# Reordering the decode part of a hybrid decoder step, with half of each decode score sum moved to GpSimd

## The chip, the cores and the metric

The kernel runs on one NeuronCore of a Trainium2 chip. The metric is the device time of one execution in microseconds. The kernel before took 907.06 us (median of three runs, 905.66 to 908.23). The profile is one further execution: 907.18 us in all, of which 905.4 us is the span from its first to its last instruction.

## What is computed

One layer of a decoder, for a prompt of 512 tokens and, in the same launch, for 8 sample tokens (one new token each, with a key/value cache of 2048 rows). Cut to what matters:

```python
proj = x_ext @ w_in                                   # 1024 -> 3*512 attention columns + RWKV columns
att  = dilated_window_attention(q, k_all, v_all)      # 8 heads; cache rows with strides 1, 4 and 16
def step(S, inp):                                     # RWKV-7, 8 heads of 64, one token after the other
    sa = einsum('bhvk,bhk->bhv', S, -kk_t)
    S  = S * w_t + sa * (kk_t * a_t) + v_t * k_t
    return S, einsum('bhvk,bhk->bhv', S, r_t)
y_rw  = (group_norm(y) * gn_w + gn_b + bonus * v) * g
x1    = layer_norm(ALPHA * x + concat(att, y_rw) @ w_out)
y     = layer_norm(ALPHA * x1 + conv_ffn(x1))
```

The samples' attention needs, for each of the 8 samples, the dot products of its query with its gathered keys (three tiles of 128 rows, 8 heads of 64 columns), a softmax, and the weighted sum of its values.

## The kernel before, in words

It is one hand-ordered program: each engine has its own list of instructions, written out in the order in which it runs, and semaphores join them. There is no scheduler. Four stages follow each other.

1. Projection (to about 222 us): 27 slots of weights, TensorE nearly always busy.
2. The recurrence by chunks (about 222 to 382 us). The 512 tokens are four pairs of chunks of 64, `n` = 0 to 3 (the text calls them the first to the fourth pair). For each pair a triangular matrix is inverted in five levels, `l` = 1 to 5. A level is a ring between TensorE and VectorE: `half_products` (TensorE, into `banks`), `halves` (VectorE, `lower<-banks,level`), `full_products` (TensorE), `update` (VectorE, `xx<-xx,banks`, and `xf<-xx,banks` in level 5). The work on pair `n - 1` that follows its inverse (`value_side`, `solved`, `step_terms`, `value_terms`, `chain_step`, `state_outputs` on TensorE; `transitions`, `chain_state`, `add_y` on VectorE; `b1_copy`, `wu_copy`, `ny_copy` on ScalarE) stands between the levels of pair `n`. At the end of a pair, `inverse_start` (VectorE, `lower<-banks,causal`), `start_inverse` (TensorE) and `x0_copy` (ScalarE) prepare the next pair; `to_tokens` (TensorE) and `token_copy` (ScalarE) transpose its keys through PSUM bank 6.
3. The output projection with the group norm beside it (about 382 to 450 us for the attention half): 16 blocks `attn_out(t)` on TensorE, each added into `z` by `attn_sum(t)`. `attn_part` says which output rows and which half of the tokens a block has. Its weights come through a ring of two: `late_high(l)` on ScalarE makes the high part, `w_low(l)` on GpSimd the low part.
4. The FFN and the norms to the end.

The decode part is strewn over stage 2. For sample `b`, the sync engine's queue loads the keys into one of three buffers (`keys_of`, which waits until `s_score(b - 3)` has freed it) and the query (`query`). GpSimd multiplies keys and query in place (`products`, L694). VectorE sums each head's 64 products (`s_score`, L1432, `sscore<-kv`). With all eight done: `decode_scores`, `s_shifted`, the exponential, `s_scaled`, `decode_back`, then `decode_values(v)` on TensorE, six groups of four products against value rows that `values_of(v)` loads through two buffers. Beside it GpSimd updates the samples' RWKV state in seven steps (`step`, L705); `state_sum(0)` and `state_sum(1)` on VectorE (L1462, `ssa<-swt`) reduce it, the first before the last five steps, the second after them. The sync queue is in order too: behind the rows that wait for `state_sum(1)` (L639) stand the first weights of stage 3 (L513), the value rows for `decode_values(2)` to `(5)` (L557 to L562), and `z` (L647, L649).

## Time and profile before

| what | value |
|---|---|
| median of three runs | 907.06 us |
| profiled execution | 907.18 us, span 905.4 us |
| TensorE busy | 829.2 us (92% of the span) |
| VectorE, ScalarE, GpSimd busy | 503.1, 330.7, 259.1 us |
| granted TensorE clock, mean | 0.960 |
| bytes read from HBM | 75.87 MB |

In the page, busy time is a share of the span over all stages. The strip of 40 slices shows where TensorE is not full: slices 12 to 17 carry the digits 7, 7, 7, 7, 5 and 8, slices 22 and 23 the digits 8 and 7, and nearly all others a 9. Slices 12 to 17 (249 to 385 us) are the recurrence, slices 22 and 23 the first norm. In rows of the timeline the columns are start, duration, engine, line, operation, tiles and shapes, count, and in brackets the idle time before with what ended it.

### The profile page before, as it was taken

The page shows a single profiled execution, that of the slowest core. Times are in us where ns is not written, and L with a number is a line of the kernel's source. Part 1 is how long each engine was busy: PE and PEld are TensorE (multiplying, and loading weights), DVE is VectorE, ACT ScalarE, POOL GpSimd, SP SyncE. Part 2 cuts the span into 40 slices and gives each one's busy share as a digit, 9 for nine tenths or more (in the row PEclk, how much of TensorE's full clock was granted, in tenths as well). Part 3 has the DMA queues.
Part 4 walks back from the last instruction along what each step waited for, and adds up shares of the span by engine and source line. Part 5 has one row for each costly group of instructions (what it writes and reads, how often), then busy time and mean ns, then how long its engine had stood idle before and what let it go on. Part 6 is the DMA issues. An engine that isn't in the chain of part 4 may idle for free.

```text
span 905.4 us, 23127 instructions
## 1 busy us (share of the span) xinstructions
PE 829.2 (92%) x10012; PEld 776.0 (86%) x10012; DVE 503.1 (56%) x764; ACT 330.7 (37%) x569; POOL 259.1 (29%) x113
## 2 busy tenths in 40 slices
PE   6999999999977775899998799999999999999994
PEld 6899889888766664688987799999999999999994
DVE  5579677685658654425643477766666662000036
ACT  5644555553321212323325633333333332111124
POOL 0000000001456440214523355444444444334300
PEclk9999999999997989899998699999999999999997
DMA  8232222242535043421221033323332322223302
GB/s 260 79 93 70 92 73 72 93 155 48 141 93 163 4 131 114 133 99 53 65 85 49 24 104 109 93 93 93 94 94 94 93 88 85 85 88 95 92 2 95
DMA packets 32470, 83.47 MB, mean 92 GB/s; under 512 B 5144, under 2 KB 10456, under 8 KB 31728
## 3 DMA queue, kind: packets, MB, share of 16 engines
q1 hardware_dynamic: 32368, 81.98, 29.3%
q8 instruction: 79, 1.29, 0.6%
q14 instruction: 23, 0.19, 0.1%
HBM read 75.87 MB, written 5.91 MB: 90 GB/s over the span
## 4 chain that ended last, share of the span: by engine, by line
PE 84%; DVE 9%; ACT 3%; issue 2%; DMA 1%; SPq 1%; POOL 0%; DVEq 0%; ACTq 0%; POOLq 0%
PE banks L1796 82%; DVE sscore L1432 1%; DVE xx L1200 1%; DVE z L1203 1%; PE banks L1850 1%; DVE rw L1200 1%; DMA kv<-in_cv 1%; PE banks L2190 1%; DVE z L1200 1%; DMA att<-in_x 1%; DVE ms L1200 1%; DVE lower L1200 1%; DVE ssa L1462 1%; DVE x_lo L1200 0%; ACT x_hi L1108 0%
## 5 line engine op out<-in xcount | busy, mean ns | idle before, releaser
L1796 PE MATMUL banks<-x_hi,w_hi 128*128 128x264 f32 (+1 forms) x784 | 208.8, 299 | 14.4 <-DVE x_lo L1200 11.5
L1796 PE MATMUL banks<-x_hi,w_lo 128*128 128x264 f32 (+1 forms) x784 | 199.3, 287 | 0.0
L1796 PE MATMUL banks<-x_lo,w_hi 128*128 128x264 f32 (+1 forms) x784 | 199.2, 287 | 0.0
L1796 PEld LDWEIGHTS banks<-x_hi,w_hi 128*128 128x128 f32 x784 | 139.9, 192 | 27.5 <-issue 15.2
L676 POOL TENSOR_TENSOR w_lo<-w_raw,w_hi 128x1024 fp32r<-128x1024 f32 (+1 forms) x40 | 95.3, 2383 | 188.9 <-ACT w_hi L791 188.7
L1796 PEld LDWEIGHTS banks<-x_lo,w_hi 128*128 128x128 f32 x784 | 140.2, 193 | 0.1
L1796 PEld LDWEIGHTS banks<-x_hi,w_lo 128*128 128x128 f32 x784 | 140.0, 192 | 0.0
L676 POOL TENSOR_TENSOR wx_lo<-w_raw,wx_hi 128x1024 fp32r<-128x1024 f32 (+1 forms) x36 | 86.1, 2393 | 101.1 <-ACT wx_hi L791 100.7
L1203 DVE SCALAR_TENSOR_TENSOR z<-z,banks 128x260 f32<-128x260 f32 (+1 forms) x24 | 12.4, 516 | 118.8 <-PE banks L1796 113.3
L1796 PE MATMUL banks<-xx,lower 64*64 64x64 f32 x1280 | 56.0, 236 | 20.3 <-DVE xx L1200 16.8
L1796 PEld LDWEIGHTS banks<-xx,lower 64*64 64x64 f32 x1280 | 49.0, 146 | 29.8 <-issue 16.4
L1796 PE MATMUL banks<-x_hi,wx_hi 128*128 128x260 f32 x352 | 73.6, 283 | 0.0
L1796 PE MATMUL banks<-x_hi,wx_lo 128*128 128x260 f32 x352 | 73.5, 283 | 0.0
L1796 PE MATMUL banks<-x_lo,wx_hi 128*128 128x260 f32 x352 | 73.4, 283 | 0.0
L1203 DVE SCALAR_TENSOR_TENSOR cv<-gp,par,cv 128x544 f32<-128x544 f32 x44 | 68.3, 1553 | 1.6
L685 POOL MEMSET kv<- 32x1536 f32 x3 | 4.1, 1372 | 219.7 <-PE banks L1796 219.5
L1200 DVE TENSOR_TENSOR h_lo<-hh,h_hi 128x520 fp32r<-128x520 f32 x22 | 51.5, 2339 | 23.7 <-ACT h_hi L1145 23.7
L791 ACT ACTIVATE w_hi<-w_raw 128x1024 fp32r<-128x1024 f32 (+1 forms) x40 | 41.6, 1039 | 45.8 <-PE banks L1796 44.9
L1796 PEld LDWEIGHTS banks<-x_hi,wx_hi 128*128 128x128 f32 x352 | 55.4, 188 | 0.2
L1796 PEld LDWEIGHTS banks<-x_hi,wx_lo 128*128 128x128 f32 x352 | 55.4, 188 | 0.0
L1796 PEld LDWEIGHTS banks<-x_lo,wx_hi 128*128 128x128 f32 x352 | 55.2, 188 | 0.0
L791 ACT ACTIVATE wx_hi<-w_raw 128x1024 fp32r<-128x1024 f32 (+1 forms) x36 | 37.3, 1037 | 46.5 <-PE banks L1796 44.8
(257 smaller groups left out, 1721.2 us busy)
## 6 DMA issues: line engine op xcount, KB each, us to landing
w_raw<-in_w SPq DMA_DIRECT2D x87, 512.0 KB, 3.6
w_raw<-in_w SPq DMA_DIRECT2D x16, 448.0 KB, 3.4
kv<-in_ck SPq DMA_DIRECT2D x16, 192.0 KB, 3.4
kv<-in_cv SPq DMA_DIRECT2D x16, 192.0 KB, 3.6
att<-in_x SPq DMA_DIRECT2D x8, 264.0 KB, 6.3
att_out<-att SPq DMA_DIRECT2D x1, 2112.0 KB, 9.0
z<-in_xc SPq DMA_DIRECT2D x2, 1040.0 KB, 9.5
y_out<-z SPq DMA_DIRECT2D x8, 260.0 KB, 2.2
```

Of the source, the lines that this page charges most:

```text
L676: pool.tensor_tensor(lo[:, 0:n * P], w_raw[:, s % 2, 0:n * P], hi[:, 0:n * P].bitcast(F32), ALU.subtract)\
L685: pool.memset(kv[96:P, r * NSB * AW:(r + 1) * NSB * AW], 0.0).then_inc(kv_zero, 1)
L791: ac.activation(w_at(l)[0][:, 0:n * P], w_raw[:, s % 2, 0:n * P], ACT.Copy).then_inc(w_hi_ready, 1)
L1200: return ve.tensor_tensor(out, a0, a1, op)
L1203: return ve.scalar_tensor_tensor(out, a0, s, a1, op0, op1)
L1432: ve.tensor_reduce(sscore[:, :, b * H:(b + 1) * H], kv[:, r * NSB * AW:(r + 1) * NSB * AW].rearrange("p (t h d) -> p t h d", t=NSB, d=HD), ...
L1462: ve.tensor_reduce(ssa[:, i, :], swt[:, :, :], AX, ALU.add).then_inc(sw_y if i else sw_sa, 1)
L1796: return pe.matmul(out, l, r, start=start, stop=stop)
L1850: ins = pe.transpose(banks[:, 4 - p, j * P:(j + 1) * P], sw[:, u % 4, j * P:(j + 1) * P], ident[:, :])
L2190: ins = pe.transpose(banks[:, 6, c * P:(c + 1) * P], x[:, c, n * P:n * P + P], ident[:, :])
```

## The change

It computes the same. On GpSimd each product is followed by a second instruction that adds the upper 32 columns of each head onto the lower 32, and VectorE sums 32 values in place of 64. The eight sums move: two to the end of the first pair, three to the end of the second, one each into levels 2, 3 and 5 of the third. The bonus products (`bonus`) go two at a time into levels 3 and 4 of the first pair, with banks of their own; the bias on ScalarE that follows them moves into the next pair. `state_sum(0)` moves from the third pair to level 3 of the second, `state_sum(1)` from level 2 of the fourth to level 3; the softmax moves from the third pair into the fourth. `transitions` and `value_terms` move back by one place each, `chain_state` to level 5 and after the last update. At a pair's end the first half of the next inverse starts before the second transposition, and the three transpositions come in another order. `decode_values(0)` to `(2)` stand in the fourth pair, `(3)` to `(5)` in stage 3. The queue loads `z` before the value rows. In stage 3 the blocks run through four output rows of one half, then four of the other.

```diff
-J_V, J_K, J_KK, J_R = (3 + i * CC for i in range(4))
+J_V, J_KK, J_K, J_R = (3 + i * CC for i in range(4))
@@ attn_part
-        return 2 * (t // 4) + t % 2, t // 2 % 2
+        return 4 * (t // 8) + t % 4, t // 4 % 2
@@ sync
-        for v in range(2, 6):
-            values_of(v)
         sp.wait_ge(bt_ps, 3 * TB - 2)
         sp.dma_start(z[:, 0:CC, :], a["xc"][:, 0:CC, :]).then_inc(z_landed, 16)
+        values_of(2)
+        values_of(3)
         sp.wait_ge(bt_ps, 3 * TB - 1)
         sp.dma_start(z[:, CC:KT, :], a["xc"][:, CC:KT, :]).then_inc(zb_landed, 16)
+        values_of(4)
+        values_of(5)
@@ gpsimd, products
-                .then_inc(s_prod, 1)
+                .then_inc(q_used, 1)
+            own(q_used)
+            x = kv[:, r * NSB * AW:(r + 1) * NSB * AW].rearrange("p (g d) -> p g d", d=HD)
+            pool.tensor_tensor(x[:, :, 0:HD // 2], x[:, :, 0:HD // 2], x[:, :, HD // 2:HD], ALU.add).then_inc(s_prod, 1)
@@ scalar, late_high
-                ac.wait_ge(o_ps, min(4 * (l - 1), 2 * KT))
+                ac.wait_ge(o_ps, (6, 8, 14, 16, 2 * KT, 2 * KT)[l - 2] if l < L_RW + 2 else 2 * KT)
@@ scalar, pairs
+            if n < TB - 1:
+                token_copy(n, 0)
+                x0_copy(n + 1, 0)
+                token_copy(n, 1)
+                x0_copy(n + 1, 1)
+                token_copy(n, 2)
...
+        ac.activation(rw[:, J_G:J_G + 2, :], rw[:, J_G:J_G + 2, :], ACT.Sigmoid).then_inc(lo_act, 1)
@@ vector, pairs
-                if (n, l) == (0, 5):
-                    s_score(0)
-                if n == 1:
-                    s_score(l)
-                if (n, l) == (2, 1):
+                if n >= 1 and l == 4:
+                    transitions(n - 1)
+                if (n, l) == (1, 3):
                     state_sum(0)
-                if n == 2 and l in (2, 3):
-                    s_score(l + 4)
-                if (n, l) == (2, 4):
+                if n == 2 and l in (2, 3, 5):
+                    s_score((5, 6, 6, 7)[l - 2])
+                if (n, l) == (3, 1):
                     s_shifted()
                 if (n, l) == (3, 2):
+                    s_scaled()
+                if (n, l) == (3, 3):
                     state_sum(1)
...
             if n >= 1:
+                chain_state(2 * n - 1)
                 add_y(n - 1)
+            if n == 0:
+                s_score(0)
+                s_score(1)
+            if n == 1:
+                s_score(2)
+                s_score(3)
+                s_score(4)
@@ tensor, end of a pair
+            if n < TB - 1:
+                inverse_scores(n + 1, 0)
+                to_tokens(n, 0)
+                full_products(n, NLEV - 1, 0)
+                inverse_scores(n + 1, 1)
+                if n >= 1:
+                    chain_step(2 * n - 1)
+                full_products(n, NLEV - 1, 1)
+                start_inverse(n + 1, 0)
+                to_tokens(n, 1)
+                if n >= 1:
+                    state_outputs(n - 1)
+                start_inverse(n + 1, 1)
+                to_tokens(n, 2)
+                if n == 2:
+                    decode_scores()
```

VectorE, from level 5 of the first pair to level 1 of the second, in the kernel before:

```order
L1432 TENSOR_REDUCE sscore<-kv 128x3x8
L1200 TENSOR_TENSOR xf<-xx,banks 128x256
L1200 TENSOR_TENSOR lower<-banks,causal 128x2x2x128
L1200 TENSOR_TENSOR xf<-xx,banks 128x256
L1200 TENSOR_TENSOR lower<-banks,causal 128x2x2x128
L1200 TENSOR_TENSOR rw<-banks,rw 128x528
L1200 TENSOR_TENSOR lower<-banks,level 128x4x64 x2
```

The same place on VectorE in the kernel after:

```order
L1214 TENSOR_TENSOR xf<-xx,banks 128x256
L1214 TENSOR_TENSOR lower<-banks,causal 128x2x2x128
L1214 TENSOR_TENSOR xf<-xx,banks 128x256
L1214 TENSOR_TENSOR lower<-banks,causal 128x2x2x128
L1447 TENSOR_REDUCE sscore<-kv 128x3x8 x2
L1214 TENSOR_TENSOR lower<-banks,level 128x4x64 x2
```

The sum `sscore<-kv` stood ahead of the last update; now two stand behind it, and the last bonus row (`rw<-banks,rw`) is gone from the end.

VectorE in the kernel after, from level 5 of the second pair into level 1 of the third:

```order
L1417 COPY carry<-nv 128x256
L1214 TENSOR_TENSOR xf<-xx,banks 128x256
L1214 TENSOR_TENSOR lower<-banks,causal 128x2x2x128
L1214 TENSOR_TENSOR xf<-xx,banks 128x256
L1214 TENSOR_TENSOR lower<-banks,causal 128x2x2x128
L1217 SCALAR_TENSOR_TENSOR carry<-banks,dec,nv 128x64 x4
L1214 TENSOR_TENSOR yy<-yy,banks 128x4x64
L1447 TENSOR_REDUCE sscore<-kv 128x3x8 x3
L1214 TENSOR_TENSOR lower<-banks,level 128x4x64 x2
```

In the kernel before each of the five levels of this pair had one such sum, and none stood at its end.

ScalarE in stage 3 of the kernel before, from the square of the first group-norm unit to its root (`w_hi` is `late_high(2)`, `gsd` the root):

```order
L1053 ACTIVATE mixa_hi<-banks 128x4x8
L1057 ACTIVATE yy<-banks 128x4x8
L1031 ACTIVATE gsq<-banks 128x512
L949 ACTIVATE nv<-banks,dec 128x64 x8
L954 ACTIVATE yy<-banks 128x4x64 x2
L791 ACTIVATE w_hi<-w_raw 128x1024
L1040 ACT_TABLE_LOAD
L1040 ACTIVATE gsd<-banks,par 128x128
```

The same in the kernel after:

```order
L1045 ACTIVATE gsq<-banks 128x512
L954 ACTIVATE nv<-banks,dec 128x64 x8
L959 ACTIVATE yy<-banks 128x4x64 x2
L1069 ACTIVATE mixa_hi<-banks 128x4x8
L797 ACTIVATE w_hi<-w_raw 128x1024
L1054 ACT_TABLE_LOAD
L1054 ACTIVATE gsd<-banks,par 128x128
```

The samples' attention rows (`mixa_hi`) now stand behind the ten copies of the last pair (`nv`, `yy`), directly ahead of `w_hi`, which in its turn waits for six output blocks in place of four.

## Rows read from the trace of the kernel before

**Rows 1.** Page: what ended last, by engine and by line.
```profile
PE 84%; DVE 9%; ACT 3%; issue 2%; DMA 1%; SPq 1%; POOL 0%; DVEq 0%; ACTq 0%; POOLq 0%
```
**Rows 2.** Windows: span; busy of PE, PEld, DVE, ACT, POOL; clock; DMA share; GB/s.
```profile
253.00:288.00 35.00, 23.51 (x787) 21.14 (x785) 21.08 (x31) 7.21 (x17) 18.26 (x6) 0.85 0.36 112
288.00:329.00 41.00, 29.53 (x958) 26.61 (x953) 27.08 (x43) 9.14 (x24) 25.71 (x7) 0.88 0.36 105
```
**Rows 3.** Waits of PE, 222 to 480 us: total, times, longest.
```profile
PE banks L1796 <- DVE xx L1200: 16.8, 12, 3.8
PE banks L1796 <- DMA kv<-in_cv: 9.2, 1, 9.2
PE banks L1796 <- issue: 4.1, 5, 1.8
```
**Rows 4.** Timeline of DVE, first to second pair.
```profile
251.41 0.42 DVE L1200 TENSOR_TENSOR xf<-xx,banks 128x256 f32<-128x256 f32 x1
...
262.35 0.42 DVE L1200 TENSOR_TENSOR lower<-banks,level 128x256 f32<-128x256 f32 x1 [7.87 <-PE banks L1796]
```
**Rows 5.** DVE groups by form, 222 to 382 us: count, busy and mean, idle.
```profile
L1432 DVE TENSOR_REDUCE sscore<-kv 128x24 f32<-128x1536 f32 x8 | 14.0, 1753 | 0.3
L1462 DVE TENSOR_REDUCE ssa<-swt 128x32 f32<-128x2048 f32 x2 | 4.6, 2286 | 0.1
```
**Rows 6.** Timeline of DVE, third pair.
```profile
300.12 0.42 DVE L1200 TENSOR_TENSOR lower<-banks,level 128x256 f32<-128x256 f32 x1 [3.35 <-PE banks L1796]
...
317.87 1.41 DVE L1200 TENSOR_TENSOR xx<-xx,banks 128x512 f32<-128x512 f32 x2
...
325.93 0.69 DVE L1200 TENSOR_TENSOR xx<-xx,banks 128x512 f32<-128x512 f32 x1 [2.75 <-PE banks L1796]
328.52 0.69 DVE L1200 TENSOR_TENSOR xx<-xx,banks 128x512 f32<-128x512 f32 x1 [1.90 <-PE banks L1796]
...
341.91 0.42 DVE L1200 TENSOR_TENSOR lower<-banks,level 128x256 f32<-128x256 f32 x1 [3.08 <-PE banks L1796]
```
**Rows 7.** Timeline of DVE, fourth pair.
```profile
367.14 0.69 DVE L1200 TENSOR_TENSOR xx<-xx,banks 128x512 f32<-128x512 f32 x1 [11.82 <-PE banks L1796]
...
381.49 0.69 DVE L1200 TENSOR_TENSOR yy<-yy,banks 128x512 f32<-128x512 f32 x1 [1.44 <-PE banks L1796]
```
**Rows 8.** Windows around the wait for the value rows, columns as in rows 2.
```profile
353.00:364.00 11.00, 1.78 (x94) 1.66 (x91) 1.05 (x3) 0.00 (x0) 0.00 (x0) 0.76 0.87 260
```
**Rows 9.** POOL groups by form, 222 to 400 us, columns as in rows 5.
```profile
L694 POOL TENSOR_TENSOR kv<-kv,qs 128x1536 f32<-128x1536 f32 x8 | 27.6, 3447 | 32.1 <-DMA kv<-srow 22.0 <-issue 9.5 <-DMA qs<-q_rows 0.5
L705 POOL TENSOR_TENSOR swt<-w_raw,svec 128x2048 f32<-128x2048 f32 x2 | 9.2, 4603 | 1.0 <-DMA sval<-sixr 0.9
L676 POOL TENSOR_TENSOR w_lo<-w_raw,w_hi 128x1024 fp32r<-128x1024 f32 x2 | 4.8, 2391 | 50.6 <-ACT w_hi L791 50.5
L734 POOL TENSOR_TENSOR gw_gate<-gsb,rw 128x512 f32<-128x512 f32 x1 | 1.3, 1265 | 0.1
```
**Rows 10.** Timeline of SP and POOL, keys of sample 4 and its product.
```profile
267.18 0.35 SPq L529 DMA_DIRECT2D kv<-in_ck  x1
272.00 3.44 POOL L694 TENSOR_TENSOR kv<-kv,qs 128x1536 f32<-128x1536 f32 x1 [9.53 <-issue]
```
**Rows 11.** Timeline of ACT and PE, stage 3.
```profile
396.19 0.43 PE L1796 MATMUL banks<-mixa_hi,w_hi 128*128 128x260 f32 x1 [0.73 <-DVE mixa_lo L1200]
...
404.31 1.89 ACT L949 ACTIVATE nv<-banks,dec 128x64 f32<-128x64 f32 x8 [1.46 <-PE banks L1796]
...
407.06 1.06 ACT L791 ACTIVATE w_hi<-w_raw 128x1024 fp32r<-128x1024 f32 x1
...
410.96 0.79 PE L1796 MATMUL banks<-grs,gsel 128*128 128x128 f32 x5 [1.00 <-issue]
```
**Rows 12.** Timeline of DVE and POOL, 439 to 443 us.
```profile
439.59 2.40 POOL L676 TENSOR_TENSOR w_lo<-w_raw,w_hi 128x1024 fp32r<-128x1024 f32 x1 [3.01 <-ACT w_hi L791]
440.20 2.34 DVE L1200 TENSOR_TENSOR gyc<-gyc,gw_gate 128x512 f32<-128x512 f32 x1
```

214 lines of the change are left out of this document (108 added, 106 removed).

## The prediction

> **What bounds the kernel now.** I read the chain that ended last first: 84% of it is TensorE [rows 1], so only time in which TensorE stands idle, or in which its work is stretched, can be won. The windows say where that is: TensorE is busy 23.5 of 35 us from 253 to 288 and 29.5 of 41 us from 288 to 329 [rows 2]. No engine is full there: VectorE has 21.1 and 27.1 us. It is a ring, TensorE and VectorE waiting for each other in turn, so whatever VectorE does between `halves` and `update` is paid in full. The waits confirm it: 16.8 us of TensorE's idle time end with `xx` of VectorE, 9.2 us in one piece with the value rows, 4.1 us with nothing that the profile shows [rows 3]. In the fourth pair VectorE then waits 11.8 us for TensorE [rows 7], and in that stretch the DMA engines move 260 GB/s at a share of 0.87 [rows 8]: it is a real queue of bytes, started late, not a slow transfer. The change works almost wholly inside the recurrence, so I walk through its four pairs from mark to mark (the first `halves` of a pair on VectorE) and then through stage 3.
>
> **Prices.** A sum of 1536 values takes 1.753 us and one of 2048 takes 2.286 us [rows 5], 1.04 ns for each value more; 768 values then take 0.95 us. The half addition on GpSimd handles 768 values; it is not in the trace. The 128x512 row takes 1.27 us and the 128x1024 row 2.39 us [rows 9], which are its bounds; halfway, and by the product's rate (3.447 us for 1536), it is about 1.75 us. Eight are 14 us more on GpSimd, beside other engines' work. A sample's keys take 4.8 us from the first issue (267.18) to the start of the product (272.00) [rows 10].
>
> **First pair to second.** The last `xf` starts its chain at 251.41 and the second pair at 262.35, after VectorE has been idle for 7.87 us [rows 4]. That idle time is a detour: bonus 3 on VectorE, its bias on ScalarE, only then the token copies, and only behind them the next inverse. All of that leaves the path. The bonus products cost TensorE the same, two at a time; with the sum of 1.75 us gone from level 5, `xf` comes at about the old time (I take 0.9 us later, since two bonus products of some 1.1 us each now stand ahead of one `half_products`). From `xf` to the next mark I take 4.7 us: two updates with their masks 2.3 us and the 3.1 to 3.4 us that VectorE waits at the other pair ends [rows 6], less 0.9 us because the two halves of the start overlap. The mark moves from 262.35 to 257.0: 5.3 us won. The two half sums (1.9 us) fit into that wait.
>
> **Second pair (37.8 us, 262.35 to 300.12).** Five sums of 1.753 + 0.03 us go: 8.9 us. `state_sum(0)` comes in, 2.3 us [rows 5]. Three half sums stand at the end, 2.9 us. The wait there was 3.35 us [rows 6], but with the last `chain_state` (0.9 us) behind the update too and the next inverse begun sooner, only about 1 us of cover is left: 1.9 us are paid. Moving `transitions` under the wait for `full_products` gives 1.9 us. Sum: 6.6 us won, 31.2 us left. If all three were covered it would be 8.5 us.
>
> **Third pair (41.8 us, 300.12 to 341.91).** `state_sum(0)` goes, 2.3 us. Two sums become three half sums: 3.5 us against 2.9 us, 0.6 us. The softmax steps go to the fourth pair, 1.7 us. The keys of samples 5, 6 and 7 can only be fetched once the sums at the end of the second pair have freed their buffers. That gives product 5 at about +4.8 us, and its halves after 3.45 + 1.75 us: 10.0 us behind the first of the three sums. VectorE reaches `s_score(5)` 2 x 0.95 + 3.0 + 4.3 = 9.2 us behind it, so it waits 0.9 us; the next two products (5.2 us each) keep pace with a level of 5.2 us. What is left is level 4: from the third `update` (317.87) to the fourth it takes 8.06 us, and the fourth's second half comes 2.6 us later still (328.52) [rows 6], because `transitions` stands ahead of `halves` and `value_terms` ahead of `full_products`. With both moved, level 4 is 1.41 + 0.1 + 0.9 + 1.85 = 4.3 us; `value_terms` is then paid before level 5, about 2 us. Together with `chain_state` out of the start of level 5 I take 7.8 us. Sum: 2.3 + 0.6 + 1.7 - 0.9 + 7.8 = 11.5 us won, 30.3 us left.
>
> **Fourth pair (39.6 us, 341.91 to 381.49).** The 11.8 us of waiting go [rows 7]. It is covered now because sums, steps and `state_sum(1)` end some 17 us sooner and because `decode_values(2)` stands behind the pair's last level. Behind `state_sum(1)` the queue now has two weights (1.05 MB), half of `z` (1.04 MB) and the value rows (0.79 MB): 2.9 MB at 260 GB/s [rows 8] are 11 us, after 1.5 us for the issues, so the rows land 13 us after the sum. TensorE comes to them 4.3 + 10 us behind it: just covered, with about 1 us to spare. To pay: the softmax, 1.7 us, and 0.5 us for its second step. That step (`s_scaled`) reads and writes only SBUF, and the GpSimd steps run beside it. One row shows what that can cost: `gyc<-gyc,gw_gate` takes 2.34 us and ends just behind `w_lo` of GpSimd [rows 12], where it otherwise takes 0.69 us. The bounds are 0 and one whole step, 4.6 us [rows 9]. Sum: 11.8 - 1.7 - 0.5 = 9.6 us won.
>
> The Trainium skill, SBUF — State Buffer, "Who interferes with whom", says that VectorE and GpSimd share one pair of ports as an exclusive lock, which a scalar operation in a two-port mode or an instruction with two SBUF inputs takes, while a reduction never does. By it the half sums stay free of the longer GpSimd work and only `s_scaled` can be held; by a rule without the lock the fourth pair would be 0.5 us shorter. The trace agrees for the row of 2.34 us.
>
> The four together: 5.3 + 6.6 + 11.5 + 9.6 = 33.0 us.
>
> **Stage 3.** Here I see losses. TensorE's fourth to sixth value group (one of them new here) adds 1.0 us. `mixa_hi` now stands on ScalarE behind the ten copies of the last pair (1.89 + 0.8 us) [rows 11], and the fifth block waits for it: about 2.1 us against the 0.73 us of the third block before. Then `late_high(2)` (1.06 us) waits for six blocks, not four, and the first root stands behind it. `gn_spread(0)`, which follows the sixth block on TensorE, waited 1.00 us [rows 11]. Now the chain is weight copy 1.06, table load 1.28, root 0.37, reciprocal 0.95 us = 3.7 us behind the sixth block, with about 1 us of `chain_step` and `state_outputs` over it: 2.8 us. Sum: 1.0 + (2.1 - 0.7) + (2.8 - 1.0) = 4.2 us lost. `z` comes sooner, which ends a wait of VectorE alone. The later weights come at about the old places.
>
> **The clock.** My walk takes TensorE's rows at 2.4 GHz. The granted clock was 0.85 and 0.88 in the two windows [rows 2], that is, part of them ran at 1.2 GHz, each time after a stretch in which TensorE had little to do; such stretches will remain. `value_terms` is now on the path in three pairs, and at 1.2 GHz it is some 2 us longer. And 1.8 us of unexplained waiting once stood in the third pair [rows 3]. I take 4 us off (bounds 0 and 10).
>
> Result: 33.0 - 4.2 - 4 = 24.8 us. The profiled execution's 907.18 us (0.12 us from the median of 907.06 us) becomes 882.4 us; I forecast 882.
>
> **Rivals.**
> 1. *The ring closes wholly.* Dense work keeps the clock at 2.4 GHz and the ScalarE waits in stage 3 are absorbed: 33.0 us, 874 us. For it: the longest idle stretches, before which the clock fell, are those that go. Against it: the waits on `xx` of 3.8 us [rows 3] come before level 2, which the change leaves as it is.
> 2. *The wait moves on.* The value rows arrive late after all, behind 1.04 MB of `z` more, or the reordered levels in the third pair bring only half of their 7.8 us. Losing 4 us there, 4 us in the third pair and 5 us more to the clock leaves 12 us: about 895 us. For it: my cover for the rows is 1 us; the 7.8 us are measured in a stretch that also had a slow clock.
> 3. *GpSimd becomes the bound, and the kernel is slower.* VectorE runs in order, so if product and half addition are slow, it stands at `s_score(5)`, `(6)` and `(7)` in levels 2, 3 and 5 of the third pair with all levels queued behind it, and each microsecond more for a half addition is paid three times. From 1.75 + 24.8 / 3 = 10 us for one half addition on the kernel is slower than before; at 12 us it would be 913 us. For it: nothing but that the operation (two inputs from one tile, in strips of 32) is not in the trace. Against it: rows of comparable size take 1.27 to 2.39 us [rows 9].
> 4. *The change does not do what it says*: the three sums at the end stop the chain for all of their 2.9 us and the other sums wait for their products, so that moving wins nothing. Even then the first pair, level 4 and the wait for value rows are left; this lies within rival 2.
>
> **How the numbers follow.** Forecast, 876 to 889 us: 0.60. Rival 1, under 876: 0.15. Rivals 2 and 4, 889 to 904: 0.18. Rival 3, slower: 0.05. No change within 0.3% (2.7 us, about what a measurement of this kernel can tell from none): 0.02. So faster 0.93, same 0.02, slower 0.05. The range reaches to 871 us, which takes in most of rival 1, and to 896 us, most of rival 2; it leaves out about 0.15.
>
> **What would show it.** After: VectorE idle between the last `xf` of the first pair and the next `halves` about 2 us instead of 7.9; sums of 0.95 us; half additions of 1.75 us; pairs of 31, 30 and 30 us; no wait over 2 us on value rows; the third pair's `s_score(5)` waiting about 1 us for GpSimd; two waits of TensorE of 2 to 3 us in stage 3; the projection and the FFN unchanged. I am wrong if a wait on `kv` or `sscore` of more than 5 us appears, or if the third pair is still over 35 us.

## The result, and the profile after

The changed kernel took 894.07 us (median of four, 892.27 to 897.88), the kernel before 907.19 us beside it: a ratio of 0.9862, 95% interval 0.9825 to 0.9899. I had forecast 882 us. The kernel is faster by 13.1 us, about half of the 24.8 us that I had worked out; the interval shows a gain of 1.0 to 1.8%. What came is the size of rival 2 ("the wait moves on", 895 us).

The profiled execution took 897.88 us (span 896.1), 9.3 us less than before's 907.18. A second profile of the same kernel, e1_after, shows 892.73 us (span 890.9); where the two differ I give both. The walk by the forecast's marks:

| us | before | forecast | after | e1_after |
|---|---|---|---|---|
| mark of the second pair | 262.35 | 257.0 | 257.80 | 256.96 |
| second pair | 37.8 | 31.2 | 34.1 | 32.0 |
| third pair | 41.8 | 30.3 | 38.6 | 38.3 |
| fourth pair, to the last `yy` | 39.6 | 30.0 | 33.6 | 32.0 |
| stage 3, to the first `lst<-banks` | 77.5 | 81.7 | 85.9 | 86.1 |
| the rest | 446.4 | 446.4 | 446.1 | 445.6 |

Each mark but the first and last is a row `lower<-banks,level` of VectorE. The first row of the table came true, the second within the spread of two profiles; the third pair and stage 3 did not. The profiled execution was forecast at 882.4 us. Of the 15.5 us by which it missed, the third pair has 8.3, stage 3 4.2, the fourth pair 3.6 and the second 2.9, less the 4 us that I had set aside for the clock.

The chain that ended last, answering to [rows 1]; the shares by engine:

```profile
PE 84%; DVE 6%; issue 5%; ACT 4%; POOL 1%; DMA 0%; DVEq 0%; ACTq 0%; POOLq 0%
```

VectorE's share fell from 9% to 6%, as wanted, but "issue" rose from 2% to 5%. TensorE's waits from 222 to 480 us [rows 3] say the same:

```profile
PE banks L1813 <- DVE xx L1214: 14.6, 11, 4.6
PE banks L1813 <- issue: 11.6, 8, 2.5
...
PE banks L1813 <- DVE z L1217: 1.3, 1, 1.3
...
PE banks L1813 <- DVE mixa_lo L1214: 1.0, 1, 1.0
PE banks L1813 <- DVE grs L1561: 0.9, 1, 0.9
PE banks L1813 <- ACT gsq L1045: 0.9, 1, 0.9
```

The 9.2 us for value rows are gone. 11.6 us now end with nothing that the profile names, where it was 4.1 us, and the last four rows are stage 3's (at 387 us, and from 424 to 428 us). The same windows as [rows 2], then that of [rows 8]:

```profile
253.00:288.00 35.00, 27.64 (x965) 24.43 (x962) 22.43 (x41) 11.18 (x24) 18.67 (x6) 0.95 0.20 57
288.00:329.00 41.00, 28.92 (x1008) 26.59 (x1003) 24.43 (x46) 7.95 (x20) 32.37 (x11) 0.88 0.42 128
353.00:364.00 11.00, 8.58 (x204) 6.98 (x195) 3.35 (x12) 5.34 (x13) 4.79 (x2) 0.84 1.02 340
```

TensorE is busier in the first of them (27.6 us against 23.5) and no busier in the second (28.9 against 29.5), where its clock is still 0.88 on average. In the third it works beside the transfers, where it stood before.

VectorE at the end of the first pair [rows 4] and the sums [rows 5]:

```profile
253.28 0.42 DVE L1214 TENSOR_TENSOR xf<-xx,banks 128x256 f32<-128x256 f32 x1 [0.18 <-PE banks L1813]
253.73 0.69 DVE L1214 TENSOR_TENSOR lower<-banks,causal 128x512 f32<-128x512 f32 x1
254.46 1.94 DVE L1447 TENSOR_REDUCE sscore<-kv 128x24 f32<-128x768 f32 x2
257.80 0.89 DVE L1214 TENSOR_TENSOR lower<-banks,level 128x256 f32<-128x256 f32 x2 [1.40 <-PE banks L1813]
```
```profile
L1447 DVE TENSOR_REDUCE sscore<-kv 128x24 f32<-128x768 f32 x8 | 7.6, 953 | 3.4 <-POOL kv L701 3.2
```

The idle time of 7.87 us has become 1.40 us, and a sum takes 0.953 us (0.95 forecast). The third pair [rows 6]:

```profile
288.92 2.93 DVE L1447 TENSOR_REDUCE sscore<-kv 128x24 f32<-128x768 f32 x3
291.88 0.88 DVE L1214 TENSOR_TENSOR lower<-banks,level 128x256 f32<-128x256 f32 x2
...
297.63 0.42 DVE L1214 TENSOR_TENSOR ms<-banks,causal 128x256 f32<-128x256 f32 x1
301.26 0.95 DVE L1447 TENSOR_REDUCE sscore<-kv 128x24 f32<-128x768 f32 x1 [3.21 <-POOL kv L701]
...
320.24 0.89 DVE L1214 TENSOR_TENSOR lower<-banks,level 128x256 f32<-128x256 f32 x2 [3.60 <-PE banks L1813]
```

The reader is to see two things: no idle time ahead of 291.88, so the three sums are partly paid, and 3.21 us at the sum of sample 5. The other side of that wait, on the sync queue and on GpSimd [rows 9, 10]:

```profile
289.94 0.35 SPq L530 DMA_DIRECT2D kv<-in_ck  x1
```
```profile
295.85 3.45 POOL L697 TENSOR_TENSOR kv<-kv,qs 128x1536 f32<-128x1536 f32 x1 [23.79 <-issue]
299.38 1.78 POOL L701 TENSOR_TENSOR kv<-kv 128x768 f32<-128x768 f32 x1
```

The keys are asked for when the first of the three sums has ended (289.87), and the product starts 5.9 us later. The half addition takes 1.78 us (1.75 forecast). TensorE's clock in the same pair, columns as in [rows 2]:

```profile
299.70:303.00 3.30, 0.01 (x2) 0.01 (x2) 1.67 (x3) 0.00 (x0) 3.22 (x2) 0.69 0.59 157
303.00:307.70 4.70, 4.70 (x136) 4.70 (x139) 1.56 (x4) 0.00 (x0) 4.54 (x3) 0.50 1.01 297
```

TensorE stands through the whole of the first window. It had stopped at 298.44 already and goes on at 302.99, 4.6 us in all (the longest of the waits on `xx` above). The granted clock fell to 0.50, its 1.2 GHz, at 301.0, while it stood, and stayed there until 307.8, so that the 4.8 us of work behind the wait ran at it. The fourth pair [rows 7]:

```profile
340.05 0.41 DVE L1463 TENSOR_SCALAR qs<-qs,sstat 64x384 f32<-64x384 f32 x1
...
351.48 1.41 DVE L1214 TENSOR_TENSOR xx<-xx,banks 128x512 f32<-128x512 f32 x2
358.60 0.89 DVE L1214 TENSOR_TENSOR lower<-banks,level 128x256 f32<-128x256 f32 x2 [5.71 <-PE banks L1813]
...
364.10 0.69 DVE L1214 TENSOR_TENSOR yy<-yy,banks 128x512 f32<-128x512 f32 x1
```

The 11.82 us wait is now one of 5.71 us at level 5, and 2.42 of these are TensorE's own unexplained wait:

```profile
358.05 0.91 PE L1813 MATMUL banks<-xx,lower 64*64 64x64 f32 x22 [2.42 <-issue]
```

Stage 3 [rows 11], TensorE's two waits and ScalarE between them:

```profile
387.42 0.56 PE L1813 MATMUL banks<-mixa_hi,w_hi 128*128 128x260 f32 x1 [1.03 <-DVE mixa_lo L1214]
...
397.56 1.13 PE L1813 MATMUL banks<-grs,gsel 128*128 128x128 f32 x8 [2.47 <-issue]
```
```profile
386.43 0.20 ACT L1069 ACTIVATE mixa_hi<-banks 128x32 fp32r<-128x32 f32 x1
393.67 1.06 ACT L797 ACTIVATE w_hi<-w_raw 128x1024 fp32r<-128x1024 f32 x1 [7.04 <-PE banks L1813]
394.74 1.28 ACT L1054 ACT_TABLE_LOAD   x1
396.04 0.37 ACT L1054 ACTIVATE gsd<-banks,par 128x128 f32<-128x128 f32 x1
```

The 2.47 us are put down to "issue", but the chain behind them is plain: weights, table, root, then the reciprocal on VectorE. This is the loss that the forecast named (2.8 - 1.0 us). From 386.30 to 393.13 us the clock is halved as well, and there the forecast had nothing; columns as above:

```profile
386.30:393.10 6.80, 5.77 (x30) 5.45 (x27) 1.37 (x6) 0.30 (x2) 0.00 (x0) 0.50 0.01 2
```

The wait of 1.03 us lies from 386.39 to 387.42. So the clock had fallen 0.09 us before it began (0.45 us before it in e1_after), and 5.7 us of work behind it ran at half the clock. TensorE had been busy without a pause from 380 us on, part of the time with thin products: 16 products of 4 columns each took 1.95 us from 383.48 on.

### The profile page after: what moved, and what is told of

Its sections match the earlier page's. It is cut to its first block, busy times and chain, and to the rows that moved or that the text cites. A ratio compares the mean times of both kernels' runs of the same rounds, so it can differ in the third digit from the quotient of the medians.

```text
span 896.1 us, 23137 instructions
## 1 busy us (share of the span) xinstructions
PE 825.6 (92%) x10012; PEld 773.6 (86%) x10012; DVE 495.5 (55%) x764; ACT 330.8 (37%) x569; POOL 273.8 (31%) x121
## 4 chain that ended last, share of the span: by engine, by line
PE 84%; DVE 6%; issue 5%; ACT 4%; POOL 1%; DMA 0%; DVEq 0%; ACTq 0%; POOLq 0%
PE banks L1813 81%; PE banks L1867 1%; ACT z L1125 1%; ACT x_hi L1122 1%; DVE xx L1214 1%; DVE z L1214 1%; DVE rw L1214 1%; DVE z L1217 1%; PE banks L2216 1%; DVE ms L1214 1%; ACT z L1185 0%; DMA w_raw<-in_w 0%; POOL kv L697 0%; DVE lower L1214 0%; POOL x_lo L749 0%
## 5 line engine op out<-in xcount | busy, mean ns | idle before, releaser
L679 POOL TENSOR_TENSOR wx_lo<-w_raw,wx_hi 128x1024 fp32r<-128x1024 f32 (+1 forms) x36 | 86.1, 2392 | 102.3 <-ACT wx_hi L797 101.9
```

What stands on the lines that cost most here:

```text
L679: pool.tensor_tensor(lo[:, 0:n * P], w_raw[:, s % 2, 0:n * P], hi[:, 0:n * P].bitcast(F32), ALU.subtract)\
```

## A wait that the profile calls issue

Of 11.6 us only the 2.47 us above are explained by a semaphore. For the others I looked at the queue that the profile's table lists as "q8 instruction", beside the data queue, as a share of the same 16 DMA engines. It moves packets of 16384 bytes: 79 packets in the whole program. The views of the transfers in two neighbouring stretches of after, first 347.2 to 355.4 us, then 355.4 to 356.6 us (kind: packets, MB, share of the engines):

```profile
q1 hardware_dynamic: 589, 2.17, 72.3%
```
```profile
q1 hardware_dynamic: 204, 0.36, 98.4%
q8 instruction: 1, 0.02, 5.2%
```

No such packet moves while 2.17 MB of weights and `z` do, then one does (355.52 to 356.51), and TensorE resumes at 358.05, 1.54 us later. In the profiles of all kernels here there are 89 waits of this kind of more than 0.25 us between 222 and 382 us; in each, TensorE resumes 1.22 to 1.70 us behind the end of such a packet. It looked as if TensorE ran out of instructions. The experiments e6, e9 and e10 are about that.

## The experiments

All are edits of the changed kernel, except e16. Each was timed beside the kernel before, whose medians were 905.9 to 906.6 us. The spread of one kernel over a handful of runs is 2 to 10 us, so a part is judged by its stretch of the profile, and the whole by the ratio.

**e1_after**: the changed kernel again.

> The changed kernel once more, beside the three that follow, so that they are compared on one chip. Both theories expect 892 to 898 us. The late-keys theory expects VectorE to wait about 3.2 us for GpSimd ahead of the sum of sample 5 again. The bytes theory expects the waits of TensorE that end with nothing the profile shows (1.98 us near 310, 2.42 us near 358) to stand at the same places.

893.19 us (892.0 to 893.7), ratio 0.9853 [0.983, 0.9877]. The third pair and stage 3 repeat to 0.3 us; the second and fourth differ by 2.1 and 1.6 us between the two profiles.

**e2_spread**: the sums of samples 2 and 3 go into levels 1 and 2 of the second pair.

```diff
+                if n == 1 and l in (1, 2):
+                    s_score(l + 1)
...
             if n == 1:
-                s_score(2)
-                s_score(3)
                 s_score(4)
```

> In the second pair the sums of samples 2 and 3 stand in levels 1 and 2 and only sample 4's at the end; all else as in the changed kernel. Theory A (late keys: the three sums at the end free the key buffers too late, VectorE waits 3.2 us at sample 5, TensorE idles 4.5 us and its clock is halved for 6.8 us after it): the second pair pays 2 x 0.98 us in its levels and gets about 2 us back at its end; product 5 comes some 25 us sooner, the wait of 3.2 us goes, the slow stretch after it too; the third pair falls from 38.6 to 32 to 34 us and the kernel is 4 to 6 us faster. Rival B (bytes: the third pair is long because TensorE's instructions arrive late behind loads): the third pair stays at 36 us or more, the kernel gains at most 2 us.

891.07 us (890.72 to 897.05), ratio 0.9845 [0.9817, 0.9873]. The wait at sample 5 is gone:

```profile
297.08 0.42 DVE L1214 TENSOR_TENSOR ms<-banks,causal 128x256 f32<-128x256 f32 x1
297.54 0.95 DVE L1447 TENSOR_REDUCE sscore<-kv 128x24 f32<-128x768 f32 x1
```
```profile
290.47:323.02 32.55, 25.02 (x981) 22.45 (x976) 21.15 (x42) 7.42 (x19) 26.17 (x7) 1.00 0.36 112
```

The third pair takes 32.55 us in place of 38.3 to 38.6, at a clock of 1.00 throughout (0.87 in after, 0.91 in e1_after): 5.7 to 6.0 us less, and 32.5 to 33.1 us in the three later kernels with this edit. This is the main error of the forecast. Counted from the start of the pair, VectorE comes to the sum of sample 5 2.3 us sooner than in after (3.4 than in e1_after), and from that sum to the end of the pair 3.7 us (2.4) are won behind it. That second part holds the halved clock and also TensorE's waits for instructions, which are 1.8 us in this pair against 3.2 and 2.5.

The edit takes away the wait and two of the three sums ahead of it at once, and the wait alone isn't the whole cause. In e7_dv below the clock falls early in the pair already (it is 0.75 from 293 to 300 us), the wait is short, and the pair still takes 38.6 us:

```profile
298.36 0.95 DVE L1447 TENSOR_REDUCE sscore<-kv 128x24 f32<-128x768 f32 x1 [1.08 <-POOL kv L701]
```

The whole kernel was expected 4 to 6 us faster and the medians show 2.1, with intervals that overlap those of e1_after. The fourth pair takes 34.1 us (33.6 and 32.0 without the edit), with an unexplained wait of TensorE of 3.4 us instead of 2.3 to 2.4, and stage 3 0.5 to 0.7 us more.

**e3_root**: `gn_root(0)` stands ahead of `late_high(2)` on ScalarE.

```diff
-        late_high(2)
         gn_root(0)
+        late_high(2)
         gn_high(0)
```

> On ScalarE the first root of the group norm stands ahead of the third weight's high part, not behind it. Theory A (stage 3 loses because the root waits for six output blocks): the reciprocal no longer ends 2.5 us of TensorE's idle time, 3 to 4 us are won. Rival B (other work fills the place, or the weight then comes late): under 1 us.

893.18 us (887.52 to 897.21), ratio 0.9841 [0.9805, 0.9877]. Stage 3 goes from 85.9 to 82.7 us in the profile and the 2.47 us wait is gone. The whole kernel doesn't show the 3 to 4 us expected: the median is that of e1_after, with six runs spread over 9.7 us.

**e4_loads**: the gate weights are issued behind the state rows, and the first half of `z` behind the value rows.

```diff
-        sp.dma_start(gate_up[:], a["gate_up"]).then_inc(gate_landed, 16)
...
         values_of(2)
         values_of(3)
         sp.wait_ge(bt_ps, 3 * TB - 1)
+        sp.dma_start(z[:, 0:CC, :], a["xc"][:, 0:CC, :]).then_inc(z_landed, 16)
```

> Only the order of loads is changed: the gate weights and two selectors (1 MB) are loaded behind the first two groups of value rows instead of behind the last keys, and the first half of z (1.04 MB) behind the value rows of groups 2 and 3 and the second transposition of the fourth pair. Theory A (bytes: the loads in one burst delay the fetch of TensorE's instructions): the waits of 1.98 us near 310 and of 2.42 us near 358 that nothing in the profile ends shrink below 0.7 us each, 3 to 5 us are won, unless z is then late. Rival B (these waits belong to TensorE's own stream): they stay at 1 to 2.5 us wherever the loads stand, and the time is the same within 1 us.

893.68 us (891.77 to 897.31), ratio 0.9863 [0.9838, 0.9889]: no change. The wait of 1.98 us near 310 us is gone, and the third pair still takes 37.6 us; that of the fourth pair stays (2.97 us, with 1.82 MB ahead of the packet): two weight tiles and the value rows do what `z` did.

**e5_fullsum**: no half additions, sums of 64 values.

```diff
-                .then_inc(q_used, 1)
-            own(q_used)
-            x = kv[:, r * NSB * AW:(r + 1) * NSB * AW].rearrange("p (g d) -> p g d", d=HD)
-            pool.tensor_tensor(x[:, :, 0:HD // 2], x[:, :, 0:HD // 2], x[:, :, HD // 2:HD], ALU.add).then_inc(s_prod, 1)
+                .then_inc(s_prod, 1)
```

> The reordered kernel without the half additions: GpSimd does the product alone, VectorE sums 64 values again (1.75 us a sum in place of 0.95). It isolates what the half sums on GpSimd bring. Theory A (what I hold: the ring pays each sum that VectorE does between its masks and updates, and the third pair waits for the product of sample 5, whose keys can only be fetched once the three sums have ended): the three sums at the end of the second pair cost 2.4 us more, and the keys of sample 5 are fetched 0.8 us later at the first free buffer; product 5 is ready 1.8 us sooner behind its keys because the half addition is gone, so the wait of 3.2 us at the sum of sample 5 goes down to about 3.2 - 1.8 + 0.8 - 2.4, nothing; the three sums in the third pair cost 2.4 us more. Second and third pair together 2.4 + 2.4 - 3.2 = 1.6 us longer, the first pair 1.6 less its cover: 0 to 1.6 us. Total +1.5 to +3 us against the reordered kernel, about 895 us against 893.5. Theory B (the half sums carry the gain, GpSimd's work is hidden): 8 x 0.8 = 6.4 us longer, 900 us. Theory C (the half additions hold the chain: the product chain of GpSimd is the bound of the third pair): it is faster, 890 us.

897.04 us (895.84 to 897.46), ratio 0.9892 [0.9862, 0.9921], 3 to 4 us above the changed kernel; the intervals of the ratios just overlap. The wait for GpSimd at sample 5 is gone, and the third pair is 37.4 us, at a clock of 0.82. The time lies between theory A (895 us) and B (900), nearer to A; C (890) is out.

**e6_shift and e9_half**: the first group of value scores is computed nine times and five times in place of once, which moves everything behind it against the edges of TensorE's packets.

```diff
-            for c in range(CC):
+            for c in [i for _ in range(9 if (n, p) == (0, 0) else 1) for i in range(CC)]:
```

> The reordered kernel with the first group of value scores of the first pair computed nine times in place of once on TensorE: 64 matrix products of 64x64 more, all before the second pair, same result. They cost 3 to 6 us in the first pair and do nothing for the rest. Theory F (the waits of TensorE that end with nothing the profile shows are waits for the next packet of its instructions, of 16384 bytes, that is for each 128 pairs of weight load and product): the places of the packets move by half a packet against the program, so the waits of 2.0 us at 310, 1.2 us at 319, 1.2 us at 333 and 2.4 us at 358 are gone from the instructions before which they stood, others stand some 64 products earlier in the program, and each still ends 1.3 to 1.6 us behind the end of such a packet. Rival G (these waits are for semaphores or a data transfer which the profile does not attribute): they stand before the same instructions as before, of the same size within 0.3 us.

The wait near 310 us stands before the same instruction, and so do those near 319, 333 and 358 us. But I had counted 64 more products, and the page shows 128 (10140 for 10012) and 80 packets for 79. That is one packet for 256 instructions, 64 bytes each, and the edges lay where they had lain: the run could not tell the theories apart. It did give the size of a packet. So I ran it again with half of that.

> The reordered kernel with the first group of value scores of the first pair computed five times in place of once on TensorE. The run with nine had 128 more pairs of weight load and product (10140 against 10012), that is one whole packet of 16384 bytes more (80 against 79), so the packets' edges lay at the same instructions again and it told nothing. Here it is 64 pairs more: half a packet. Theory F (TensorE's unexplained waits stand at the edges of its instruction packets): the waits inside value_terms of the third pair and before the last products xx,lower of levels 3 and 5, which stood before the same instructions in both earlier runs, are gone from there; waits of 0.5 to 3 us stand 64 pairs earlier or later in the program, each ending 1.3 to 1.6 us behind the end of a packet. Rival G (a semaphore or a transfer): same instructions as before.

894.1 us, one run. With 64 products more, TensorE's waits from 305 to 312 us are

```profile
PE banks L1813 <- DVE xx L1214: 1.1, 1, 1.1
```

in place of, in after,

```profile
PE banks L1813 <- issue: 2.0, 1, 2.0
PE banks L1813 <- DVE xx L1214: 0.4, 1, 0.4
```

The wait inside `value_terms` near 319 us has gone as well; others of 0.43 and 0.94 us have come at 318.7 and 324.2 us, before `rw,aa` and `level,lower`, where none stood. A wait of 1.60 us at 357.83 is also before an `xx,lower`, but not before the one of after: it is the 5288th product of the program, where that of after (358.05) is the 5161st and would be the 5225th here. Numbered by product modulo 128, all 89 waits stand at places 59 down to 31, the later in the program the lower, and none anywhere else. No semaphore and no data has changed, only the count of instructions ahead. Rival G falls: these waits are TensorE waiting for its next 256 instructions.

**e7_dv**: the first two value groups of the fourth pair go behind the `half_products` of levels 4 and 5.

```diff
+                if n == 3 and l >= 4:
+                    decode_values(l - 4)
...
-                    decode_values(0)
-                if (n, l) == (3, 4):
-                    decode_values(1)
```

> The reordered kernel, but the first two groups of the value products of the samples in the fourth pair stand behind the half_products of levels 4 and 5 in place of ahead of them, so that VectorE can work beside them. Theory P (in the ring a value group of about 1.0 us ahead of half_products is paid in full, behind it it lies beside VectorE's masks): the fourth pair is 1 to 2 us shorter than in the reordered kernel and VectorE's wait of 5.7 us at level 5 shrinks to 4 to 5 us. Rival F2 (the fourth pair is bound by the instruction packets of TensorE that wait behind the bulk transfers): the pair keeps its length within 0.5 us since the packet comes no sooner. Total 892.5 us by the first, 893.5 by the second.

897.34 us (893.24 to 898.41), ratio 0.9891 [0.9858, 0.9923]. The fourth pair takes 35.0 us, not less; TensorE's wait for instructions is 3.46 us where it was 2.42. Theory P is wrong here. I read it so that what TensorE does ahead of the packet is cover for it; no run shows that by itself.

**e8_terms**: `value_terms` goes behind `half_products` of level 5 in three pairs.

```diff
-                if n >= 1 and l == 4:
+                if n >= 1 and l == 5:
                     if n >= 2:
                         chain_step(2 * n - 2)
                     value_terms(n - 1)
```

> The reordered kernel, but value_terms (128 products of 64x64, about 2.1 us at full clock) and the chain step ahead of it stand behind half_products of level 5 in place of ahead of it, in the second, third and fourth pair. Theory P (what my forecast had: where value_terms stands it is paid before level 5, about 2 us a pair, here 1 to 1.5 us a pair of it lie beside VectorE's two masks of level 5): 3 to 4.5 us faster, about 889.5 us; each of the three pairs is 1 to 1.5 us shorter. Rival Q (chain_state stands ahead of VectorE's last updates and waits for the copies of value_terms on ScalarE, so a later value_terms only moves the wait from the masks to that place): the time stays within 1 us.

903.51 us (898.79 to 907.87), ratio 0.9973 [0.9949, 0.9997]: 10 us slower than the changed kernel, which neither theory had. The place is Q's, the size is not:

```profile
360.70 0.86 DVE L1217 SCALAR_TENSOR_TENSOR carry<-banks,dec,nv 128x64 f32<-128x64 f32 x4 [7.44 <-ACT nv L954]
```

`chain_state` needs the copies `nv` of ScalarE, which need the whole of `value_terms`; with it behind `half_products`, VectorE stands for it for 3.5, 1.8 and 7.4 us in the three pairs. Of the 7.4 us, 4.0 are a wait of TensorE for instructions inside `value_terms`, so not all of the loss is the order's own. The pairs take 35.8, 36.5 and 38.3 us: the second and the fourth are longer, the third is 2 us shorter. Of the two places tried, that of the changed kernel is the cheaper one.

**e10_throttle**: the sync queue waits for each of the two late weight tiles before it goes on.

```diff
-        weights(N_IN)
-        weights(N_IN + 1)
+        for l in range(2):
+            weights(N_IN + l)
+            sp.wait_ge(w_landed[(N_IN + l) % 2], 16 * ((N_IN + l) // 2 + 1))
```

> The reordered kernel with one thing more: in the fourth pair the sync queue waits for the first late weight tile (0.52 MB) to land before it issues the second, and for the second before it goes on to z and the value rows. The same bytes are moved. Theory F (the packet with TensorE's next instructions is served only behind the bytes that are queued ahead of it: 2.2 MB between the packets at 347.0 and 355.5, DMA engines full from 350 on): the packet comes about 3 us sooner, the wait of 2.4 us before the products of level 5 is gone or under 1 us, and the halved clock behind it is shorter; the fourth pair is 2 to 4 us shorter than 33.6 (32.0 in the second run of the same kernel), total 1 to 3 us less than the reordered kernel's 893.5, unless the value rows come later than decode_values(2) needs them. Rival H (TensorE stood there for the masks of level 5 anyway, the packet is hidden by that): the fourth pair stays within 1 us, and the value rows, 1 to 2 us later, may cost that much.

900.36 us (897.05 to 903.75), ratio 0.9934 [0.9909, 0.9959]: slower than the changed kernel. But the fourth pair takes 29.66 us, what the forecast had. TensorE from 347 to 358 us:

```profile
PE banks L1814 <- DVE rw L1215: 1.2, 1, 1.2
PE banks L1814 <- DVE xx L1215: 1.1, 1, 1.1
PE banks L2217 <- ACT yy L960: 0.5, 1, 0.5
```

No "issue" is left, with the same bytes in the same order. The packet that moved at 355.52 in after moves at 352.33 here. So Theory F's other half holds too: the packet is late when the bulk data is queued ahead of it. What is won is then lost at the value rows, which come late behind tiles and `z`:

```profile
365.79 1.94 PE L1814 MATMUL banks<-kv,sprob 128*32 128x512 f32 x8 [5.72 <-DMA kv<-in_cv]
```

The changed kernel has no such wait, so my cover for these rows held there, and this used it up. Stage 3 takes 96.0 us in place of 85.9: more than the 5.7 us, with the clock at 0.50 from 361.8 to 372.0 us.

**e11_sums**: e3_root, and the samples' sums stand ahead of `value_terms` on TensorE, `mixa_hi` ahead of the ten copies on ScalarE, `mixa_lo` ahead of `chain_state` on VectorE.

```diff
         attn_out(3)
-        value_terms(TB - 1)
         decode_sums()
+        value_terms(TB - 1)
...
         gn_square(0)
-        ny_copy(TB - 1)
         ac.wait_ge(s_sum, 1)
...
         own(s_mix_hi)
+        ny_copy(TB - 1)
```

> Stage 3 of the reordered kernel with two changes: the group norm's first root stands ahead of late_high(2) on ScalarE (as in e3_root), and the samples' attention sums stand ahead of value_terms on TensorE, with mixa_hi ahead of the ten copies on ScalarE and mixa_lo ahead of chain_state on VectorE. Theory S (my forecast's: the fifth block waits for mixa_lo because mixa_hi stands behind the ten copies of 1.89 + 0.8 us; the halved clock of the 6.7 us behind that wait follows from it): the wait of 1.0 us is gone, and with it up to 3.4 us of halved clock; stage 3 from the last add of the recurrence to the first norm goes from 82.7 us (e3_root) to 79 to 81.5 us. Rival T (the ten copies, now behind mixa_hi, hold up the chain of states and so gn_var): another wait of the same size takes its place, and stage 3 stays at 82 to 84 us.

887.02 us (885.48 to 889.69), ratio 0.9793 [0.977, 0.9816]. Stage 3:

```profile
361.11:440.54 79.43, 76.55 (x910) 66.25 (x910) 37.08 (x67) 25.11 (x45) 24.87 (x16) 0.98 0.25 79
```

79.4 us at a clock of 0.98, where e3_root had 82.7 at 0.94. With a wait of 1.0 us gone 3.3 us are won; the rest is the low clock from 386.3 us on, of which nothing is left here. That is what theory S expected (79 to 81.5 us), not T (82 to 84). But the edit also moves the thin products ahead of the wait (`par,srow`) to another place, and the clock had fallen before the wait began; which of the two the low clock belongs to isn't shown.

**e12_best**: e2, e11, e10 and the gate weights of e4 together.

> The combination: sums of samples 2 and 3 in levels 1 and 2 of the second pair (e2_spread), the root and the attention sums as in e11_sums, the gate weights issued behind the state rows (part of e4_loads), the late weights one after the other (e10_throttle). If the parts are independent: e2_spread 2 us, stage 3 3.4 to 6 us, the waits near 308 and 355 about 2 us each: 884 us, 881 to 889. Rival: each wait that goes lets another one through (fetch or clock), as in e2_spread, where 6 us won in the third pair left 2 us in all: about 889 us.

894.26 us (889.05 to 896.65), ratio 0.9857 [0.9827, 0.9886]: above both the 884 us of the parts' sum and the rival's 889. The 5.7 us for value rows are there again.

**e13_vfirst**: e11 with e10's waits, and the value rows ahead of `z`. **e14_nothrottle**: e11 with e2 and the gate weights of e4. **e15_best**: all of these.

```diff
+        values_of(2)
+        values_of(3)
         sp.wait_ge(bt_ps, 3 * TB - 2)
         sp.dma_start(z[:, 0:CC, :], a["xc"][:, 0:CC, :]).then_inc(z_landed, 16)
-        values_of(2)
-        values_of(3)
```

> e11_sums with the late weight tiles loaded one after the other as in e10_throttle, and with the value rows of the third and fourth value group ahead of the first half of z in the queue. Theory F: as in e10_throttle the packet of instructions comes in time, the wait before the products of level 5 (3.2 us in e11_sums) is gone and the fourth pair is 30 to 31.5 us (34.4 in e11_sums); the 5.7 us that TensorE stood for value rows in e10_throttle came from z (1.05 MB, 4 us) ahead of them, so 0 to 1.7 us are left. Total 884 to 886 us, against 887.0 of e11_sums. Rival: z now lands late and attn_sum(0) waits for it, which holds up TensorE's third block; the time stays at 887 or above.

892.15 us (888.51 to 894.18), ratio 0.985 [0.9822, 0.9878]. In the profile (888.83 us) the fourth pair is 29.9 us and 1.8 us of wait for value rows are left, slightly over what was expected; but stage 3 takes 83.7 us where e11 has 79.4, which is nearly all that the fourth pair had won (34.4 to 29.9), and the median is 5 us above e11's 887.02.

> e11_sums with the sums of samples 2 and 3 in levels 1 and 2 of the second pair (e2_spread) and the gate weights behind the state rows (part of e4_loads), no change to the late weights. If the parts add: third pair 32 to 34 us in place of 38, the wait before level 5 in the fourth pair stays at 2.5 to 4 us; 884 to 886 us. If the fetch gives the gain back as in e2_spread: 886 to 889 us.

886.09 us (884.54 to 888.14), ratio 0.9783 [0.9761, 0.9806]: the fastest version by its median, though no clear step from e11_sums (887.02 us): the 5.3 us won in the third pair are 0.9 us in the whole. Third pair 32.5 us, stage 3 79.4 us, the fourth pair 33.3 us with TensorE's wait of 3.2 us still in it.

> Both together: e14_nothrottle with the late weights one after the other and value rows ahead of z. Third pair 32 to 34, fourth pair 30 to 31.5, stage 3 79 to 81 us: about 881 us (878 to 885). Rival: the value rows, behind the gate weights now (0.3 us of bytes more), are waited for again by more than 2 us: 885 or more.

889.24 us (880.93 to 891.35), ratio 0.9806 [0.9772, 0.984]. The profiled execution, 880.93 us, has pairs of 32.6, 32.6 and 29.0 us; the five others took 888 to 891. Against the profile of e14_nothrottle the fourth pair wins 4.3 us and stage 3 loses 3.6 (82.95 us against 79.38), with 2.2 and 0.8 us of waits for the loads of `kv` in it. What the five others lose beyond that has no trace. So the waits on the sync queue do away with TensorE's wait for instructions before level 5 and still do not pay; a part of the loss is in stage 3, the rest stays open.

**e16_halfonly**: the kernel before with the half sums alone.

```diff
+            own(q_used)
+            x = kv[:, r * NSB * AW:(r + 1) * NSB * AW].rearrange("p (g d) -> p g d", d=HD)
+            pool.tensor_tensor(x[:, :, 0:HD // 2], x[:, :, 0:HD // 2], x[:, :, HD // 2:HD], ALU.add).then_inc(s_prod, 1)
```

> The kernel before with the half sums alone: each product on GpSimd followed by the half addition (1.80 us), each sum on VectorE of 32 values (0.95 us in place of 1.75), everything else at its old place. By the walk of my forecast: five sums in the second pair and one at the end of the first 0.8 us each, 4.8 us, and two in the third pair 1.6 us; but GpSimd's chain of steps is 14.4 us longer, state_sum(1) and with it the weights and the value rows behind it come later where the fourth pair already waited 9.2 us for them. GpSimd had 9.5 us of idle time for the products in which it waited for nothing shown, the rest is waits for keys, which come 0.8 us a sample sooner. Theory V (the value rows set the end of the recurrence in the kernel before): the rows come 2 to 6 us later, minus the 6.4 us that the sums give: the time is within 3 us of before (904 to 909). Rival W (the sums are paid one by one in the ring): 900 to 901 us.

901.56 us (898.6 to 906.48), ratio 0.9955 [0.9934, 0.9975]: 4.4 us from the half sums alone, and 3 to 4 us by e5. The second pair is 32.6 us (37.8 before), the third 40.0 (41.8); the fourth stays at 39.8 us (39.6 before) with 8.9 us of wait for value rows, but starts sooner. Rival W is the nearer. Of the 13 us, then, about 4 are the half sums' and about 9 the order's.

## Why the prediction was right in part and wrong in size

**First pair to second: right.** 5.3 us forecast, 4.6 and 5.4 measured; both sums lie in the wait.

**Second pair: nearly right.** 6.6 us forecast, 3.7 and 5.8 measured. The mark at 291.88 has no idle time ahead of it, so the three sums are paid in part, as assumed. The two profiles differ by 2.1 us, and over the seven profiles whose kernels are the same up to here the pair takes 31.0 to 35.2 us; my 31.2 is at the lower end.

**Third pair: this step failed.** I had 30.3 us and got 38.6. The wait at `s_score(5)` was sized at 0.9 us and was 3.21. VectorE came to it 9.1 us behind the start of the sums (288.92 to 298.05), as forecast (9.2). The product was late: I let the keys be fetched from the start of the first sum, but its buffer is free when it has ended, 1.0 us on, and the keys took 5.9 us and not 4.8. The step "so it waits 0.9 us" thus missed 2.3 us, 2.1 of them in these two points; and the walk had no term for what comes with such a stop. e2_spread took the wait and two of the sums ahead of it away and won 5.7 to 6.0 us. Of the 2.2 us by which its pair is still over the forecast, waits for instructions are 1.8 us (the longer two 0.43 and 1.17). Level 4 itself came as forecast: in e2_spread from its third `update` at 303.63 to its fourth at 308.18, 4.55 us against 4.3.

**Fourth pair: right in its mechanism, short by 2 to 3.6 us.** The value rows no longer hold it, `s_scaled` took 0.41 us and was not held (the GpSimd steps had ended), so its 0.5 us were nothing. What was missing is the wait for instructions behind 2.2 MB of loads, which now run beside TensorE's levels, where in the kernel before TensorE stood for the value rows anyway; e10_throttle, without that wait, shows 29.66 us against the 30.0 forecast.

**Stage 3: the mechanism right, the term half its size.** 4.2 us forecast, 8.4 measured. Root behind the weight copy: 1.8 us forecast, 3.2 by e3_root. The wait on `mixa_lo`: 2.1 us forecast, 1.03 measured, but 3.3 us by e11_sums, low clock included. The remaining loss, 79.4 us against 77.5, is 1.9 us where the new value group had 1.0.

**The clock.** I took 4 us as one lump. It comes in single stretches: 4.6 us of standing and then 4.8 us of work at 0.50 in the third pair, 5.7 us of work at 0.50 behind the wait in stage 3. In the third pair the clock fell while TensorE stood, in stage 3 just before it did. The lump of 4 us was no estimate of these.

**The rivals.** Rival 2 had the size. Its cause was another: no value row came late, and level 4 came as priced (4.55 us against 4.3; the 7.8 us as a whole no run singles out). The loss lay at the sample sums, the clock and the instructions, and that it added up to rival 2's 895 us is chance. Rival 3 was wrong in size (1.8 us, not 10), but VectorE did stand at the first of the three sums that it named. The lock on the shared ports [rows 12] shows in another row than I had looked at: the copy `carry<-nv` of 256 columns took 1.32 us in the kernel before, with GpSimd at work until 289.37 us,

```profile
288.19 1.32 DVE L1403 COPY carry<-nv 128x256 f32<-128x256 f32 x1
```

and 0.29 us in after, with GpSimd idle:

```profile
281.38 0.29 DVE L1417 COPY carry<-nv 128x256 f32<-128x256 f32 x1
```

By the Trainium skill, SBUF — State Buffer, "Who interferes with whom", a copy can take the shared ports and a reduction never does. The runs agree: the sums took 0.95 us beside GpSimd and without it.

## What to carry to other kernels

Price a wait that a change creates at more than its length: here the pair with 3.2 us of it was 6 us longer, and the stage with 1.0 us of it 3.3 us longer, with TensorE at half its clock for 4.8 and 5.7 us of work behind it. But read in the trace where the clock fell, before taking the wait for its cause. When a buffer is freed by the first of several instructions, count from that instruction's end through the whole transfer, and spread such instructions out rather than put them in one place. In a long program without loops, keep bulk loads away from places where TensorE has little cover: its instructions come through the same DMA engines. Judge such a step by the whole kernel too; here much of what one pair won was lost again in the next.

## What the runs showed of the hardware

- Instructions of TensorE arrive in packets of 16384 bytes, 256 instructions or 128 products with their weight loads (128 products more: 80 packets for 79). TensorE resumes 1.22 to 1.70 us behind the end of the packet it stands for (89 waits).
- Such a packet comes later when data is queued ahead of it. Without loads between two packets no wait was longer than 1.53 us; each of the 16 waits from 1.84 to 4.01 us had 1.50 to 2.47 MB of loads between its packet and the one before, and with the tiles issued one by one (e10_throttle) the wait of 2.4 us was gone. As many bytes don't always cost as much: 1.97 MB went with a wait of 1.20 us in e5_fullsum.
- A half addition on GpSimd, 768 values from one tile in strips of 32, took 1.80 us; the product of 1536 values 3.44 us.
- `e8_terms` shows what order can cost: 128 products moved by one place on TensorE made the kernel 10 us slower, a wait for instructions of 4.0 us included.
- The granted clock of TensorE fell to 0.50 at 386.30 us while the engine was busy by its records, with thin products among them.
